# A new order for the last strips of an fp32 residual block, and a new start of its weight stream

## What is computed

```python
def reference(x, ...):                       # x: (1, 256, 2048)
    h = rms_norm(x, pre_mix_g)
    y = hybrid_mixer(h, w_in, ...)           # begins with h @ w_in (2048 x 4416)
    x = x + rms_norm(y, post_mix_g)
    h = rms_norm(x, pre_mlp_g)
    m = jnp.square(jax.nn.relu(h @ w_up)) @ w_down      # 2048 x 8192, 8192 x 2048
    x = x + rms_norm(m, post_mlp_g)
    return x
```

## Time and profile before

| | |
|---|---|
| median of three runs | 1084.32 us |
| the profiled execution | 1082.61 us |
| its span, first to last instruction | 1080.6 us |
| TensorE busy | 1064.9 us, 99% |
| VectorE busy | 694.3 us, 64% |
| ScalarE busy | 513.4 us, 48% |
| HBM read | 204.84 MB |

### The profile page before, as it was taken

One profiled execution on the slowest core, in us unless ns is written; L12 is line 12 of the kernel. 1 busy time (PEld: TensorE's weight loads), 2 busy tenths in 40 slices (PEclk: granted clock), 3 DMA queues, 4 the chain that ended last, 5 costly groups with the idle time before them and its releaser, 6 DMA issues.

```text
span 1080.6 us, 13612 instructions
## 1 busy us (share of the span) xinstructions
PE 1064.9 (99%) x4874; PEld 885.6 (82%) x4874; DVE 694.3 (64%) x766; ACT 513.4 (48%) x655; POOL 94.1 (9%) x102
## 2 busy tenths in 40 slices
PE   9999999999999999999999999999999999999996
PEld 7888888888888788888888888888888888888875
DVE  6465565558975677575665765756657656566586
ACT  6564445445544564444444444444444444444443
POOL 0010120120000420000000000000000000000003
PEclk9999999999999999999999999999999999999999
DMA  9765455453755555666656766666576665675642
GB/s 336 277 217 181 155 167 174 146 192 131 298 195 195 156 178 183 219 201 203 214 167 230 216 201 207 190 214 214 174 234 210 204 207 171 215 234 173 237 156 78
DMA packets 114655, 214.73 MB, mean 199 GB/s; under 512 B 7232, under 2 KB 20160, under 8 KB 113856
## 3 DMA queue, kind: packets, MB, share of 16 engines
q1 hardware_dynamic: 114480, 214.27, 61.0%
q10 hardware_dynamic: 144, 0.04, 0.0%
HBM read 204.84 MB, written 2.10 MB: 192 GB/s over the span
## 4 chain that ended last, share of the span: by engine, by line
PE 93%; DVE 3%; ACT 1%; issue 1%; POOL 1%; DMA 0%; SPq 0%; DVEq 0%; POOLq 0%; ACTq 0%
PE ps L635 30%; PE ps L637 30%; PE ps L636 30%; PE ps L643 2%; DVE w_lo L1182 1%; DVE aT_raw L1223 1%; DMA raw<-in_w_in 0%; PE ps L817 0%; DVE acc L1242 0%; PE ps L871 0%; PE ps L822 0%; DVE xT_lo L1408 0%; ACT u_sb L1004 0%; POOL x_res L1629 0%; ACT w_hi L917 0%
## 5 line engine op out<-in xcount | busy, mean ns | idle before, releaser
L1182 DVE TENSOR_TENSOR w_lo<-raw,w_hi 128x1024 fp32r<-128x1024 f32 (+2 forms) x383 | 470.0, 1235 | 333.9 <-ACT w_hi L917 331.4
L917 ACT ACTIVATE w_hi<-raw 128x1024 fp32r<-128x1024 f32 (+2 forms) x383 | 397.2, 1039 | 468.9 <-PE ps L637 461.3
L635 PE MATMUL ps<-w_hi,xT_hi 128*128 128x512 f32 (+1 forms) x800 | 313.1, 391 | 2.6 <-DVE xT_lo L1268 1.4
L637 PE MATMUL ps<-w_lo,xT_hi 128*128 128x512 f32 (+1 forms) x800 | 309.4, 387 | 0.0
L636 PE MATMUL ps<-w_hi,xT_lo 128*128 128x512 f32 (+1 forms) x800 | 309.2, 386 | 0.0
L635 PE MATMUL ps<-w_hi,yT_hi 128*128 128x512 f32 x672 | 263.1, 392 | 2.7 <-DVE yT_lo L1202 2.7
L637 PE MATMUL ps<-w_lo,yT_hi 128*128 128x512 f32 x672 | 261.7, 389 | 0.0
L636 PE MATMUL ps<-w_hi,yT_lo 128*128 128x512 f32 x672 | 261.6, 389 | 0.0
L635 PEld LDWEIGHTS ps<-w_hi,xT_hi 128*128 128x128 f32 x800 | 150.5, 188 | 35.0 <-issue 3.6
L637 PEld LDWEIGHTS ps<-w_lo,xT_hi 128*128 128x128 f32 x800 | 150.3, 188 | 30.5
L636 PEld LDWEIGHTS ps<-w_hi,xT_lo 128*128 128x128 f32 x800 | 150.5, 188 | 28.7
(11 more groups left out here) (147 smaller groups left out, 428.5 us busy)
## 6 DMA issues: line engine op xcount, KB each, us to landing
raw<-in_w_up SPq DMA_DIRECT2D x64, 1024.0 KB, 5.4
raw<-in_w_down SPq DMA_DIRECT2D x64, 1024.0 KB, 6.2
raw<-in_w_in SPq DMA_DIRECT2D x28, 1024.0 KB, 5.2
raw<-in_w_o SPq DMA_DIRECT2D x16, 1024.0 KB, 5.1
aT_raw<-a_blk SPq DMA_DIRECT2D x224, 32.0 KB, 1.9
raw<-in_w_uq SPq DMA_DIRECT2D x8, 576.0 KB, 4.0
raw<-in_w_ukv SPq DMA_DIRECT2D x4, 1024.0 KB, 5.0
raw<-in_w_in SPq DMA_DIRECT2D x7, 512.0 KB, 8.4
```

Source lines behind the costliest of these rows:

```text
L635: nc.tensor.matmul(dst, x_hi, hi, start=first, stop=False)
L637: mm = nc.tensor.matmul(dst, x_hi, lo, start=False, stop=last)
L917: nc.scalar.activation(w_hi[:, slot, 0:size], raw[:, raw_slot, first:first + size], ACT.Copy).then_inc(hi_ready, 1)
L1182: nc.vector.tensor_tensor(w_lo[:, slot, 0:size], raw[:, raw_slot, first:first + size], f32(w_hi[:, slot, 0:size]), ALU.subtract).then_inc( ...
```

## The change

At the end of the program, the loop stops one strip earlier, and the planner writes out up(14), up(15), down(13), down(14), down(15). The activations of strips 14 and 15 both go by `a_turn` and 16 DMAs. They get places of their own in `yT_hi` and `yT_lo` (chunks 4 and 8; `A_SLOT`), and up(15) gets the PSUM banks 2 and 3. At the start, the four chunks of the first quad are loaded and split one by one, the first three pieces of xT are issued on ScalarE's queue, and TensorE waits for each of the parts of a chunk by itself (`first_quad`): first hi·hi of both token blocks, then those with the weights' low part, then those with xT's low part.

```diff
+A_SLOT = {FF_STRIPS - 2: 4, FF_STRIPS - 1: 8}
@@ plan(), start
-    steps += [("split_chunk", 0, 0), ("xT", 0, 0), ("split_chunk", 1, 0), ("xT", 1, 0)]
-    for h in (1, 2, 3):
+    for c in range(4):
+        steps += [("split_chunk", c, 0), ("xT", c, 0)]
+    for h in (2, 3):
@@ plan(), tail
+    for q in range(4):
+        products(up(j - 1, q, n := n + 1), tail)
+    tail.append(("relu", j - 1, n))
     for q in range(4):
         products(up(j, q, n := n + 1), tail)
+        if q == 0:
+            tail.append(("a_turn", j - 1, 0))
     tail.append(("relu", j, n))
     for q in range(4):
-        n = down(j - 1, q, n + 1)
-        for k in range(4):
-            tail.append(("mm", n, k))
-            if k == 1 and q in (1, 2):
-                tail.append(("a_shift", j, 2 * q - 1))
+        products(down(j - 2, q, n := n + 1), tail)
+        tail.append(("add", 4 * (j - 2) + q, n))
+        if q == 0:
+            tail += [("a_turn", j, 0), ("aT", j - 1, A_SLOT[j - 1])]
+    for q in range(4):
+        products(down(j - 1, q, n := n + 1), tail)
         tail.append(("add", 4 * (j - 1) + q, n))
-        if q < 2:
-            tail.append(("a_shift", j, 2 * q))
-        if q == 2:
-            tail.append(("aT", j, 4))
+        if q == 0:
+            tail.append(("aT", j, A_SLOT[j]))
@@ the loop
-    LOOP = range(2, FF_STRIPS - 1)
+    LOOP = range(2, FF_STRIPS - 2)
@@ SyncE, start
-            for c in range(2):
-                sp.dma_start(raw[:, 0, c * W:(c + 1) * W], quad_source(0)[:, c]).then_inc(w_chunk_landed[c], 16)
-                load_xT(c)
-            load_half(0, 1, raw_landed[0])
-            load_xT(2)
+            for c in range(4):
+                sp.dma_start(raw[:, 0, c * W:(c + 1) * W], quad_source(0)[:, c]
+                             ).then_inc(w_chunk_landed[c] if c < 3 else raw_landed[0], 16)
@@ SyncE, tail
-                if n == NQ_TAIL + 2:
-
-                    sp.wait_ge(aT_lo_ready, FF_STRIPS - 2)
-                    move_blocks(FF_STRIPS - 1)
+                if n in (NQ_TAIL + 2, NQ_TAIL + 8, NQ_TAIL + 12):
+
+                    j = FF_STRIPS - {2: 3, 8: 2, 12: 1}[n - NQ_TAIL]
+                    sp.wait_ge(aT_lo_ready, j)
+                    move_blocks(j + 1)
@@ TensorE
+            def first_quad(k, wk):
+
+                hi, lo = wk
+                pe.wait_ge(hi_ready if k % 2 else chunk_hi_ready, k // 2 + 1)
+                pe.wait_ge(xT_hi_ready, k + 1)
+                for tb in range(TB):
+                    nc.tensor.matmul(ps[:, tb], blocks(xT_hi, k, tb), hi, start=k == 0, stop=False)
+                pe.wait_ge(lo_ready if k % 2 else chunk_lo_ready, k // 2 + 1)
+                for tb in range(TB):
+                    nc.tensor.matmul(ps[:, tb], blocks(xT_hi, k, tb), lo, start=False, stop=False)
+                pe.wait_ge(xT_lo_ready, k + 1)
+                for tb in range(TB):
+                    mm = nc.tensor.matmul(ps[:, tb], blocks(xT_lo, k, tb), hi, start=False, stop=False)
+                return mm
@@ ScalarE, start
+            load_xT(0)
             act.dma_start(gains[:], t["gains"]).then_inc(gains_landed, 16)
+            load_xT(1)
+            load_xT(2)
```

More of the change, by code:

```diff
@@ L367, in hybrid_block @@
         ident_landed, gains_landed = sem("ident_landed"), sem("gains_landed")
-        w_chunk_landed = [sem(f"w_chunk_landed{c}") for c in range(2)]
+        w_chunk_landed = [sem(f"w_chunk_landed{c}") for c in range(3)]
         w_first_landed = [sem(f"w_first_landed{n}") for n in range(1, RAW)]
@@ L523, in up_bank @@
         def up_bank(j):
-            return 6 if j == 1 else 0
+            return {1: 6, FF_STRIPS - 1: 2}.get(j, 0)
         def conv_bank(half, c):
@@ L667, in stream @@
                 width, kind = z["width"], z["kind"]
-                if n == 0 and k == 0:
-                    pe.wait_ge(chunk_lo_ready, 1)
-                elif k % 2 == 0 or n == 0 and k == 1:
+                if n > 0 and k % 2 == 0:
                     pe.wait_ge(lo_ready, 2 * n + k // 2 + 1)
@@ L677, in stream @@
                         wait_strip_bank(z["strip"])
-                    if z["strip"] == 0:
+                    if z["strip"] == 0 and z["q"]:
                         pe.wait_ge(xT_lo_ready, 4 * z["q"] + k + 1)
                     first, last = z["first"] and k == 0, z["last"] and k == 3
-                    mm = product(strip_bank(z["strip"]), width, (xT_hi, xT_lo), 4 * z["q"] + k, wk, first, last)
+                    if n == 0:
+                        mm = first_quad(k, wk)
+                    else:
+                        mm = product(strip_bank(z["strip"]), width, (xT_hi, xT_lo), 4 * z["q"] + k, wk, first, last)
                 elif kind == "out":
@@ L726, in stream @@
                             pe.wait_ge(hT_lo_ready, 2 * z["q"] + 2)
-                        elif z["j"] > 1 and z["q"] == 0:
+                        elif 1 < z["j"] < FF_STRIPS - 1 and z["q"] == 0:
                             pe.wait_ge(relu_ready, z["j"])
@@ L741, in stream @@
                             pe.wait_ge(relu_ready, 1 + (z["q"] > 0))
-                    at = 4 if z["j"] == FF_STRIPS - 1 else 0
+                    at = A_SLOT.get(z["j"], 0)
                     mm = product(4 + 2 * (z["q"] % 2), width, (yT_hi, yT_lo), at + k, wk, k == 0, k == 3, tbs)
@@ L951, in hidden_hi @@
                 if shifted:
-                    act.wait_ge(a_turned, j + 1)
+                    act.wait_ge(a_turned, 1)
                 else:
@@ L957, in hidden_hi, with load_xT @@
                 ins.then_inc(aT_hi_ready, 1)
+            def load_xT(part):
+                cs = slice(*XT_PARTS[part])
+                act.dma_start(xT_raw[:, cs], t["xT"][:, cs]).then_inc(xT_landed[part], 16)
+            load_xT(0)
             act.dma_start(gains[:], t["gains"]).then_inc(gains_landed, 16)
+            load_xT(1)
+            load_xT(2)
             act.wait_ge(ones_ready, 1)
@@ L969, in step @@
                 elif what == "split_chunk":
[L970 to L973, removed]
+                    act.wait_ge(w_chunk_landed[a] if a < 3 else raw_landed[0], 16)
+                    part = slice(a % 2 * W, (a % 2 + 1) * W)
+                    nc.scalar.activation(w_hi[:, a // 2, part], raw[:, 0, a * W:(a + 1) * W], ACT.Copy
+                                         ).then_inc(hi_ready if a % 2 else chunk_hi_ready, 1)
                 elif what == "xT":
@@ L1123, in step @@
                 elif what == "aT":
-                    hidden_hi(a, b, a in SHIFTED)
+                    hidden_hi(a, b, a == 0)
                 elif what == "m_square":
@@ L1258, in step @@
                 elif what == "split_chunk":
[L1259 to L1262, removed]
+                    dve.wait_ge(hi_ready if a % 2 else chunk_hi_ready, a // 2 + 1)
+                    part = slice(a % 2 * W, (a % 2 + 1) * W)
+                    nc.vector.tensor_tensor(w_lo[:, a // 2, part], raw[:, 0, a * W:(a + 1) * W],
+                                            f32(w_hi[:, a // 2, part]), ALU.subtract
+                                            ).then_inc(lo_ready if a % 2 else chunk_lo_ready, 1)
                 elif what == "xT":
@@ L1413, in step @@
                 elif what == "a_turn":
-                    turn_blocks(a, None)
+                    turn_blocks(a, (a - 1) * 256 if a > 1 else None)
                 elif what == "a_shift":
```

3 lines of the change are left out of this document (1 added, 2 removed).

## The result

The changed kernel takes 1089.75 us (median of 5 runs, 1089.22 to 1090.43); the kernel before, timed beside it, 1083.8 us (5 runs, 1082.58 to 1084.45). The ratio is 1.0056, 95% interval 1.0045 to 1.0068: slower by some 6 us. The forecast was 1089.8. The profiled execution took 1089.28 us with a span of 1087.5, 6.9 us more than the span of before. Two slow executions, one of the kernel before and one of before_fill, are left out of all medians, ranges and ratios of this document.

A forecast was written before the change was run, and what follows sets the result against it. TensorE, busy 99% of the span, was taken to bound the kernel, so only its waits count. Tail waits +4.35, low clock +2.4 and start -1.3 gave +5.45 us on the median of 1084.32: 1089.8 us, range 1085.0 to 1092.0.

The forecast's parts named there:

- quads 9 and 13: Second quads (24 matmuls each) of down(13) and down(14), numbered from up(14)'s first as 0: delays of 0.6 and 7.35 us.
- The tail's waits: Last five strips: TensorE loses 7.4 us in waits instead of 3.06, so +4.35 us, bounds +2.0 and +6.5.
- The sets: 16 activation moves each for strips 14 and 15, holding SyncE's queue 10.05 us ahead of weight loads.
- Two splits for quad 10: VectorE, third quad of down(13): both weight halves done 1.1 + 2.35 us after ScalarE takes them up, at 1013.2.
- the second set: SyncE's 16 moves after strip 15's turn and strip 14's low part: start at 1016.75, next load at 1026.8.
- The load of quad 13: Weights of down(14)'s second quad: issued at 1026.8, landed 6.1 us later at 1032.9.
- The restart: TensorE at down(14)'s second quad: resumes 4.6 us after the load lands, behind two splits and an add, at 1037.5.
- The clock: After the long wait of 6.3 us: 1.2 GHz for 5 us, costing 2.4 us, bounds 0 and 2.9.
- The start: First quad: 0.95 us from its inner order plus 0.35 from an earlier landing, -1.3 us, bounds -0.5 and -2.0.
- the clock holds: Rival for the tail: same waits, but the clock stays up or falls too late to cost much; 1087.4 us, 25%.
- Short waits: Rival for the tail: down(13)'s second quad on time, shortest chain to down(14)'s second 5.0 us; 1085.0 us, 14%.
- the moves do not hold the loads: Rival for SyncE's queue: 16 issues under about 5 us, no late weight, both waits gone; 1080.0 us, 11%.

The follow-up runs named there:

- before_fill: The kernel before with 11 matmuls into an unused bank in its end wait: 1082.64 us, ratio 0.9989 to the kernel before.
- moves_10_14: The changed kernel with each new set of 16 moves two loads further back in SyncE's queue: 1078.46 us, ratio 0.9944 to the kernel before.
- moves_pool: The changed kernel with the moves of strips 14 and 15 issued by GpSimd's queue instead of SyncE's: 1078.42 us, ratio 0.9951.
- half_moves: The changed kernel issuing 8 of each 16 moves in the same places, so its result is not the layer's: 1078.48 us, ratio 0.9951.
- fill: The changed kernel with 22 unread matmuls in the long wait behind down(14)'s first quad: 1087.7 us, ratio 1.004 to the kernel before.
- moves_10_12: The changed kernel with only the first new set of moves two loads further back: 1085.95 us, ratio 1.0012 to the kernel before.
- add_first: The changed kernel with the add of down(13)'s last quad ahead of two splits on VectorE: 1087.21 us, ratio 1.0035 to the kernel before.
- tail_only: The changed kernel's new order of the last five strips with the start of the kernel before: 1089.87 us, ratio 1.005.
- xT_on_sp: moves_10_14 with the first three pieces of xT back on SyncE's queue: 1079.03 us, ratio 0.9957 to the kernel before.
- start_only: The changed kernel's new start with the tail of the kernel before: 1083.46 us, ratio 0.9993.
- moves_8_14: The changed kernel with only the second new set of moves two loads further back: 1080.51 us, ratio 0.9969 to the kernel before.

## Why the prediction was right, and where its sizes were off

**The mechanism stands.** SyncE's queue held the loads of quads 9 and 13 behind two sets of moves, the add of quad 11 stood behind both splits of quad 13, and the clock fell in the wait. moves_10_14 and moves_pool take the hold away and keep all the moves, half_moves shortens it, and each removes every wait for a weight or an add in the tail and the whole loss.

**The tail's waits: forecast +4.35, measured +6.06** (9.12 us of waits against 3.06). Its parts can be read off:
- The sets took 11.05 and 11.25 us, not 10.05. In each, one issue took 1.6 us where the others take 0.59. An instruction fetch lies beside each such issue; the link was only seen, no run tests it.
- Two splits for quad 10 took 3.28 us, not 2.35. The first overlaps GpSimd's square of strip 15:

```profile
1010.35 3.28 DVE L1208 TENSOR_TENSOR w_lo<-raw,w_hi 128x1024 fp32r<-128x1024 f32 x2 [0.69 <-ACT w_hi L936]
...
1014.68 1.29 DVE L1239 STREAM_TRANSPOSE a_blk<-a_sb 128x512 f32<-128x512 f32 x2
```
```profile
1009.44 1.97 POOL L1558 TENSOR_TENSOR a_sb<-a_sb 128x1024 f32<-128x1024 f32 x1 [24.64 <-ACT a_sb L966]
```

  The trace of before had such a pair too, beside the square of strip 14 at 982.73, and the forecast took its 2.35 us from a pair without a square beside it:

```profile
983.63 3.21 DVE L1182 TENSOR_TENSOR w_lo<-raw,w_hi 128x1024 fp32r<-128x1024 f32 x2 [2.65 <-ACT w_hi L917]
```

  With the later first set this puts the second set at 1017.17. The forecast had 1016.75 less the start's 0.8, so it is 1.2 us late.
- The load of quad 13 landed in 5.3 us and that of quad 9 in 5.4, not 6.1: the nearest row, a load alone (5.0), was the better one. The restart came 4.73 us after it (forecast 4.6).
- Quads 10 and 11 lost 0.82 and 0.33 us where I had 0.2 for quad 11 alone, and quad 9 lost 1.07, not 0.6. I had treated the add as late only at quads 11 and 13; it stands behind splits at each down quad, and in my own chain, which ends quad 8's add at 1014.3 just before quad 10 is due, the slow split alone makes quad 10 late.

**The clock: forecast 2.4, measured 1.65** (2.05 by fill's medians). It was low for 3.4 us of matmuls, not 5. This is one execution: in the profiles of moves_10_12, add_first and tail_only the slow matmuls after the same kind of wait cost 2.3, 2.4 and 2.8 us, so the forecast lies within what the runs show. By the rule of the Trainium skill ("TensorE: Matmul & The Clock Gate", Part 1) an idle stretch brings the throttled level back; the falls after 4.4 to 7.1 us from matmul to matmul agree, and fill shows the other side: with TensorE at work in the wait the clock stayed up.

**The start: forecast -1.3, measured -0.8.** The 0.35 us that I gave to an earlier landing did not come. The first split comes at 4.30 instead of 3.67, since the table load starts 1.45 us later and the first chunk lands later too; the first matmul, whose xT waits for the gains, comes at 5.96 instead of 5.57. The bare place in the order, 0.95, was nearer. By the rule of the Trainium skill ("DMA: Bandwidth & Descriptors", Issuing engines are not separate DMA queues) a second issuer saves its issuing time only. I had taken that for nothing, though three issues of 0.43 us leave SyncE's queue. In xT_on_sp quad 1 starts 0.56 us later than in moves_10_14, which the rule allows, but this is less than the 0.69 us between profiles of one start code, so no run here decides it.

**The sum.** +6.06 + 1.65 - 0.8 = +6.9 on profiled executions against +5.45 forecast. That 1089.8 and 1089.75 agree is in part luck. The forecast had the waits too small by 1.7 us, the low clock too large by 0.75 and the start's gain too large by 0.5, which leaves it 1.45 us too low on profiled executions. The other way, the median of before from which I counted already held 1 to 1.5 us of low clock, which the changed kernel no longer has at that place, so my base was too high by about as much. Median to median the change is +5.95.

**The rivals.** That the clock holds fell with the profile. Short waits fell: the waits were longer than the central values. The 5.0 us of its shortest chain was worked out with a landing of 6.1 us, though the rival argues with the 5.0 of a load alone, which would have made it 3.9; moves_10_12, where quad 9 is on time, lost 5.57. The rival that the moves do not hold the loads needed issues of under 5 us: they took 11, and with 5 (half_moves) no weight was late. What stays open: why one issue in each set is slow, what decides whether the clock falls in a wait of about 3.1 us from matmul to matmul, and how the start's gain divides between its edits.

## What to carry to other kernels

Small DMAs with a wait of their own, in a queue that also carries loads ahead of their use, hold every load behind them for the time of the wait and of all their issues; put them behind every load whose buffer is free by then, or on the queue of an idle engine. Here two loads further back turned +6 us into -5.5. Price a new wait of some microseconds together with the slow clock behind it. Before adding a difference to a median, ask whether the profiled execution is a typical one, and before dividing half a microsecond between two edits, look how much it varies between profiles of the same code.

## What the runs showed of the hardware that was not expected

- The clock can fall after a wait of about 3 us in one execution (start_only: restart at 1049.05, low from 1049.4) and hold in another.
- GpSimd issues these 32 KB moves between partitions faster than SyncE: 16 in 7.87 to 8.06 us, some 0.50 each, against 10.28 to 11.25 (0.63 each, and a slow one in most sets).
- A VectorE split of 1.23 us took 2.1 us when it began 0.9 us after a GpSimd square of 1.97 us (3.28 or 3.29 us for two, in the changed kernel, tail_only, add_first and moves_8_14).
- Low stretches were of different length: 6.8 us in the changed kernel (1035.1 to 1041.9), 3.4 in start_only, and about 10 us in tail_only, whose wait is nearly as long as that of the changed kernel. Nine of the ten:

```profile
1035.00:1044.00 9.00, 5.28 (x13) 4.20 (x14) 8.10 (x8) 4.04 (x6) 0.00 (x0) 0.50 1.05 386
```
